# Forget attention, its output projection and the next input projection in one stage

## The chip, the cores and the metric

The kernel runs on one core of one Trainium2 chip, as one program of 18725 recorded instructions. The metric is the device time of one execution in microseconds (us); lower is better. Matrix products run on TensorE (PE, with its weight loads as PEld), elementwise work on VectorE (DVE) and ScalarE (ACT), a little on GpSimd (POOL), and the weight transfers are issued by SyncE (SP).

## The reference

Two stacks follow each other on a sequence of 256 tokens of width 1024 in float32: a two-layer one, and then four layers of the kinds fox, gla, gdn and fox again. Only the two fox layers and what follows them matter here. The mixer of such a layer is:

```python
def fox_mixer(xn, w_in, b_f, q_gain, k_gain, w_out):   # 8 heads of 128
    q, k, v, z, f_logit = split(xn @ w_in)              # 4 * 1024 + 8 columns
    q, k = rms_norm(q, q_gain), rms_norm(k, k_gain)
    cum = cumsum(log_sigmoid(f_logit + b_f), axis=1)
    logits = q @ k.T * scale + (cum[q_pos] - cum[k_pos]), -inf above the diagonal
    p = softmax(logits)
    return ((p @ v) * silu(z)) @ w_out
# the layer: x = x + mixer(rms_norm(x, norm_w)); the next layer: rms_norm(x) @ w_in of gla
```

After the second fox layer x is the result.

## The kernel before, in words

The 256 tokens are two tiles of 128 (`NT` = 2, tile t holds tokens 128t to 128t+127). `core.x` holds the residual stream on chip, and PSUM has 8 banks of 512 float32 columns for each partition.

**Products.** Every large projection is computed to near float32 accuracy from split operands: a weight and an activation are each the sum of a high part (a cast by ACT, `split_hi`, L188) and a low part (a subtraction by DVE, `split_lo`, L197), and `products` (L209 to L211) issues three matmuls, high by high, low by high and high by low. A weight comes in chunks of at most 4 x 128 rows by 512 columns, in the order in which `plan_weights` lists them. Three raw slots (`NRAW`) and three split slots (`NSPL`) exist. `issue` on SP's queue starts the transfer of a chunk when the chunk three places ahead of it has been split; `split_hi` waits for the landing, and for the products of the chunk three places back (`used`). The output projection is 4 chunks: two blocks of 512 columns, two halves of the 1024 rows each.

**Stages.** The program is a chain of stages; `core.stage` opens a block in which each engine has its own instruction list and waits on semaphores, and at its end all engines meet (L260). Around a fox layer they are:

- the stage that ends with the layer's input projection (`stage_ffn` for the first fox layer, `stage_seam` for the second). `Rest` runs its 9 blocks of 456 columns: PE multiplies, ACT moves each block out of PSUM with a scale (L934). The small steps of the layer (norms of q and k, their transposes, the gates) are hung into this loop by `fox_sides`. z is the last 1024 columns, so it lies in blocks 6 to 8.
- `stage_fox_attend`. It has four units, tile 0 heads 0 to 3, tile 0 heads 4 to 7, and the same for tile 1. Of each: PE makes the logits (L2513), DVE adds the gates and takes the row maxima (L2556) and negates them (L2561), ACT takes the exponentials with their sums (L2596), PE transposes them (L2540), DVE copies the transposes to SBUF (L2584), PE multiplies by v (L2525), DVE divides by the sums (L2570) and multiplies by silu(z) (L2575). ACT begins the stage with silu over all of z (L2591). The order on PE is written out: logits one unit ahead, values one unit behind. A unit of tile 0 sees 128 keys, a unit of tile 1 sees 256.
- the seam (`stage_seam`), for the first fox layer with the gla input projection, or `stage_last` for the second. `Turned` transposes the result of both tiles (L503), keeps PE running with three unused matmuls (`keep_warm`, L204), and ACT and DVE split the transposes in high and low (L512, L520), between the splits of the first two weight chunks. Then `Out` multiplies both blocks; its residual additions are DVE's (L579). In a seam, `Rms.pe` puts the transposes of x (L625) among products: those of tile 0 among the last products of the output projection, those of tile 1 among the first of the next projection. ACT and DVE scale and split them (L640, L647), after which `block` multiplies tile 0 and then tile 1 of the first block. ACT's list then has the squares of x (L669), POOL's power for the norm (L678), and the next weight splits.

The waits that set the order in the seam are these few:

```python
core.issue(sp, out.job[-1][-1]["g"] + 1)            # SP: the 4 chunks of the output projection
sp.wait_ge(sem("y_turn"), KD // 2)
core.issue(sp, body.job[-1][-1]["g"] + 1 + NRAW)    # then the next projection's, and 3 more
```

Of the kernel before, what the change touches and what calls it, by code (L numbers as in the profile page):

```python
# [72 lines left out]
class Core:  # L73


    def __init__(self, nc, a, ctx):
# [31 lines left out]
        self.chunks, self.jobs, self.mod = [], {}, {}  # L108
        self.issued = 0
# [347 lines left out]
class Splits:  # L457


    def __init__(self, core, names):  # L460
        self.core = core
        self.hi, self.lo = core.split_rings()
        self.chunks = [c for name in names for blk in core.jobs[name] for c in blk]
        self.at = {c["g"]: n for n, c in enumerate(self.chunks)}
        self.done = {"act": 0, "dve": 0}
# [129 lines left out]
class Norm:  # L595
# [3 lines left out]
    def __init__(self, core, tag, out, name, at):  # L599
        self.core, self.tag, self.out, self.job, self.split = core, tag, out, core.jobs[name], out.split  # L600
        self.hi, self.lo = core.act_pair()
        self.base = out.base
# [25 lines left out]
    def block(self, pe, sem, between):  # L628
        core, s = self.core, self.split
        core.mm_tiles(pe, self.job[0], s.hi, s.lo, self.hi, self.lo, lambda t: core.ps[:, 2 * self.base + t, :], 2, None,  # L630
# [50 lines left out]
class Rms(Norm):  # L681
# [8 lines left out]
    def pe(self, pe, sem):  # L690
# [6 lines left out]

        def second(t, i, j):
# [4 lines left out]
        self.out.pe(pe, sem, first)  # L703
        self.block(pe, sem, second)
# [25 lines left out]
class LnRms(Norm):  # L730
# [15 lines left out]
    def pe(self, pe, sem):  # L746
# [9 lines left out]
        self.core.keep_warm(2, 2 * self.base + 1)  # L756
# [43 lines left out]
class Ln(Norm):  # L800
# [17 lines left out]
    def pe(self, pe, sem):  # L818
# [9 lines left out]
        self.core.keep_warm(2, 2 * self.base + 1)  # L828
# [72 lines left out]
class Rest:  # L901


    def __init__(self, core, norm, dst, side, scaled):
        self.core, self.norm, self.dst, self.side, self.scaled = core, norm, dst, side, scaled
        self.split, self.job = norm.split, norm.job
# [5 lines left out]
    def bank(self, n, t):  # L912
        return 2 * ((self.norm.base + n) % 2) + t
# [11 lines left out]
    def act(self, act, sem):  # L925
        self.norm.act(act, sem)
        if self.scaled:
            act.wait_ge(self.norm.s(sem, "rms"), 1)
        for n, blk in enumerate(self.job):
            self.split.act(act, self.split.last(blk) + NSPL)  # L930
            act.wait_ge(self.core.used, blk[-1]["idx"] + 1)
            for t in range(NT):
                scale = self.norm.rs[:, t:t + 1] if self.scaled else 1.0
                self.core.nc.scalar.activation(self.dst(n, t), self.core.ps[:, self.bank(n, t), 0:blk[0]["width"]], ACT.Copy,  # L934
                                               scale=scale).then_inc(sem("taken"), 1)
            self.run("act", n, act, sem)

# [11 lines left out]
class Gated:  # L949
# [10 lines left out]
    def bank(self, n, t):  # L960
        return self.core.ps[:, 2 * ((self.norm.base + n) % 2) + t, :]
# [70 lines left out]
def stage_seam(core, before, name, scale, at, dst, side):  # L1032
# [4 lines left out]
    split = Splits(core, (prev, name))  # L1037
    out = Out(core, "y", split, prev, Turned(core, split, y))
    body = Rest(core, Rms(core, "m", out, name, scale, at), dst, side, True)
# [2578 lines left out]
```

## Time and profile before

| | |
|---|---|
| median of three runs | 1575.83 us (1567.4, 1575.83, 1576.15) |
| profiled execution, its own time | 1573.45 us |
| span of its trace | 1571.7 us |
| PE busy | 1435.2 us, 91% of the span |
| PEld, DVE, ACT, POOL busy | 73%, 56%, 44%, 14% |
| mean granted TensorE clock | 0.951 of full speed |
| products of the large projections, L209 to L211, x1216 each | 471.3, 461.4 and 462.4 us busy |
| weight splits, L188 on ACT and L197 on DVE, x176 each | 316.3 and 407.3 us busy |

The span is the time from the first to the last recorded instruction; 1.75 us of the execution lie outside it. Busy times of PE are recorded lengths that overlap (the next matmul enters before the last has left), so durations worked out from PE are taken from starts, not from recorded lengths. The granted clock is 1.00 at 2.4 GHz and 0.50 at 1.2 GHz.

### The profile page before, as it was taken

What the parts mean: (1) busy time and instruction counts of PE and PEld (TensorE: products, weight loads), DVE (VectorE), ACT (ScalarE), POOL (GpSimd) and SP (SyncE); (2) the same over time, 40 slices, a digit from 0 to 9 for tenths busy, and PEclk for the clock granted to TensorE, in tenths of its full rate; (3) what the DMA queues carried; (4) which work ended last, traced back from release to release, by engine and by line L of the source; (5) the groups of instructions that cost most, each with busy time, mean ns of one, the idle gap of its engine ahead of it and who ended that gap; (6) DMA issues with size and microseconds to landing.
All of it is one profiled execution on the core that took longest, in us unless ns stands there. A gap on an engine that the chain in (4) does not pass through costs nothing. (4 is left out here: it accounts for less than half of the span.)

```text
span 1571.7 us, 18725 instructions
## 1 busy us (share of the span) xinstructions
PE 1435.2 (91%) x7434; PEld 1145.8 (73%) x7434; DVE 875.7 (56%) x1179; ACT 689.4 (44%) x985; POOL 214.4 (14%) x119
## 2 busy tenths in 40 slices
PE   6999999999999988889999989979999974979988
PEld 2684668777888765567888868968886974868976
DVE  0755792667554553456755455646436577365635
ACT  1432432155443445346444335545543773236542
POOL 0003532103000040211200000200000032310300
PEclk7999799899999998799999999999999997989999
DMA  9655363165565463815666438805523530028821
GB/s 328 213 172 177 134 237 139 47 222 187 188 214 175 147 200 104 291 47 160 214 188 214 161 119 184 225 10 169 171 95 121 191 133 15 1 71 185 214 95 54
DMA packets 157155, 244.10 MB, mean 155 GB/s; under 512 B 14070, under 2 KB 95946, under 8 KB 156556
## 3 DMA queue, kind: packets, MB, share of 16 engines
q1 hardware_dynamic: 155916, 237.56, 48.4%
q0 software_dynamic: 1152, 5.34, 0.9%
q8 instruction: 59, 0.97, 0.2%
q14 instruction: 28, 0.23, 0.0%
HBM read 241.77 MB, written 1.11 MB: 155 GB/s over the span
## 5 line engine op out<-in xcount | busy, mean ns | idle before, releaser
L197 DVE TENSOR_TENSOR w_lo<-w_raw,w_hi 128x2048 fp32r<-128x2048 f32 (+3 forms) x176 | 407.3, 2324 | 273.0 <-ACT w_hi L188 272.9
L209 PE MATMUL ps<-w_hi,act_hi 128*128 128x512 f32 (+4 forms) x1216 | 471.3, 388 | 8.4 <-DVE act_lo L520 3.3
L211 PE MATMUL ps<-w_hi,act_lo 128*128 128x512 f32 (+4 forms) x1216 | 462.4, 380 | 0.0
L210 PE MATMUL ps<-w_lo,act_hi 128*128 128x512 f32 (+4 forms) x1216 | 461.4, 379 | 0.0
L188 ACT CAST w_hi<-w_raw 128x2048 fp32r<-128x2048 f32 (+3 forms) x176 | 316.3, 1803 | 293.9 <-PE ps L211 212.7
L209 PEld LDWEIGHTS ps<-w_hi,act_hi 128*128 128x128 f32 x1216 | 230.1, 189 | 53.3 <-issue 12.9
L211 PEld LDWEIGHTS ps<-w_hi,act_lo 128*128 128x128 f32 x1216 | 229.5, 189 | 37.3
L210 PEld LDWEIGHTS ps<-w_lo,act_hi 128*128 128x128 f32 x1216 | 230.0, 189 | 35.6 <-issue 1.4
L318 PE MATMUL ps<-w_raw,condz 128*32 128x512 f32 x384 | 63.7, 771 | 19.2 <-DMA w_raw<-in_ada_w 15.1
L934 ACT ACTIVATE proj<-ps,nstat 128x456 f32<-128x456 f32 (+2 forms) x64 | 37.1, 632 | 88.3 <-PE ps L211 88.3
L209 PE MATMUL ps<-w_hi,ffn_gh 128*128 128x512 f32 x176 | 70.2, 399 | 0.0
L211 PE MATMUL ps<-w_hi,ffn_gl 128*128 128x512 f32 x176 | 69.7, 396 | 0.0
L210 PE MATMUL ps<-w_lo,ffn_gh 128*128 128x512 f32 x176 | 69.7, 396 | 0.0
L204 PE MATMUL ps<-con 128*128 128x512 f32 x96 | 50.5, 673 | 18.3 <-DVE up L3413 18.3
L664 POOL TENSOR_TENSOR nstat<-nstat,con 128x1 f32<-128x1 f32 x8 | 5.4, 678 | 432.9 <-DVE nstat L659 432.9
L204 PEld LDWEIGHTS ps<-con 128*128 128x128 f32 x96 | 20.5, 226 | 39.1 <-issue 39.0
L326 PEld LDWEIGHTS ps<-con,ada_part 128*128 128x128 f32 x192 | 31.2, 247 | 23.6 <-issue 18.8
L336 ACT COPY ada_part<-ps 128x512 f32<-128x512 f32 x24 | 14.0, 583 | 74.4 <-PE ps L318 74.4
L1003 ACT ACTIVATE ffn_s<-ps 128x256 f32<-128x256 f32 x44 | 14.5, 381 | 68.9 <-PE ps L211 68.9
L318 PEld LDWEIGHTS ps<-w_raw,condz 128*32 128x32 f32 x384 | 10.3, 122 | 45.9 <-DMA w_raw<-in_ada_w 25.3
L211 PEld LDWEIGHTS ps<-w_hi,ffn_gl 128*128 128x128 f32 x176 | 33.2, 189 | 7.9
L210 PEld LDWEIGHTS ps<-w_lo,ffn_gh 128*128 128x128 f32 x176 | 33.2, 189 | 7.6
(478 smaller groups left out, 1838.6 us busy)
## 6 DMA issues: line engine op xcount, KB each, us to landing
w_raw<-in_ada_w SPq DMA_DIRECT2D x48, 1024.0 KB, 6.7
w_raw<-in_ffn_w_in SPq DMA_DIRECT2D x88, 512.0 KB, 4.9
w_raw<-in_fox_w_in SPq DMA_DIRECT2D x32, 912.0 KB, 9.1
w_raw<-in_ffn_w_out SPq DMA_DIRECT2D x20, 1024.0 KB, 5.1
w_raw<-in_rwkv_w_rkv SPq DMA_DIRECT2D x12, 1024.0 KB, 5.2
w_raw<-in_gla_w_in SPq DMA_DIRECT2D x10, 896.0 KB, 4.8
w_raw<-in_gdn_w_in SPq DMA_DIRECT2D x10, 896.0 KB, 5.0
w_raw<-in_fox_w_out SPq DMA_DIRECT2D x8, 1024.0 KB, 5.0
```

The lines of the kernel that those rows point to most:

```text
L188: self.nc.scalar.copy(hi[:, s, 0:c["nk"], 0:c["width"]], self.raw[:, c["slot"], 0:c["nk"], 0:c["width"]]).then_inc(self.hi_done, 1)
L197: self.nc.vector.tensor_tensor(lo[:, s, 0:c["nk"], 0:c["width"]], self.raw[:, c["slot"], 0:c["nk"], 0:c["width"]], hi[:, s, 0:c["nk"], 0:c ...
L204: self.nc.tensor.matmul(self.ps[:, bank, :], self.c("ident"), moving, start=True, stop=True)
L209: nc.tensor.matmul(out(t)[:, 0:w], xh[:, k, tok], hi[:, s, j, 0:w], start=start, stop=False)
L210: nc.tensor.matmul(out(t)[:, 0:w], xh[:, k, tok], lo[:, s, j, 0:w], start=False, stop=False)
L211: return nc.tensor.matmul(out(t)[:, 0:w], xl[:, k, tok], hi[:, s, j, 0:w], start=False, stop=stop)
L318: r = core.nc.tensor.matmul(self.sums[32 * j:32 * j + 32, :], core.condz[:, k, :], core.raw[:, c["slot"], j, :], start=(k < KG), stop=(k > ...
L326: r = core.nc.tensor.matmul(self.turned[:, 4 * n + j:4 * n + j + 1], self.part[n % 2][:, j * P:j * P + P], core.c("ones")[:, 0:1], start=T ...
L336: core.nc.scalar.copy(self.part[n % 2][:, :], self.sums).then_inc(sem("ada_part"), 1)
L664: self.core.nc.gpsimd.tensor_tensor(self.rs[:, t:t + 1], self.ve[:, t:t + 1], self.core.c("mhalf")[:, 0:1], ALU.pow).then_inc(self.s(sem, ...
L934: self.core.nc.scalar.activation(self.dst(n, t), self.core.ps[:, self.bank(n, t), 0:blk[0]["width"]], ACT.Copy, scale=scale).then_inc(sem( ...
L1003: nc.scalar.activation(self.act_s[:, n % 2, t, :], self.bank(n, t)[:, 0:T], ACT.Silu).then_inc(sem("silu"), 1)
```

## The change: one stage in place of two, and another order in it

`stage_fox_attend` is removed. Its work becomes a class, `FoxMix`, whose lists for PE, ACT and DVE are run at the head of the stage of the output projection (`stage_seam` or `stage_last`). What differs:

- All four units have logits buffers of their own (`lg` has 4 places in place of 2). PE issues the logits of all four first, then turns and values.
- `Tiles` takes the place of `Turned`: the attention's result is transposed, and split in high and low, one token tile at a time. `OutTiles` takes the place of `Out`: it multiplies in parts, one part being one chunk for one token tile (12 matmuls). Parts (0, tile 0), (1, tile 0) and (2, tile 0) stand among the attention of tile 1; the other five follow. PSUM banks are dealt out by tile.
- The first two chunks of the output weight are split already in the stage before (`ahead`), the third at the head of ACT's list in the new stage, and at the end of the mixer's DVE list.
- silu(z) is applied as the input projection is moved out of PSUM (`Rest.act`, blocks 6 to 8; block 6 is cut in two), and L2591 is gone. ACT begins the new stage with an exponential of one column.
- The transposed exponentials of the last unit are copied by ACT, not DVE.
- In the gla seam the transposes of x for tile 0 stand after all products of the output projection, followed by two unused matmuls (`keep_warm`), no longer among the last products. `OutTiles` ignores `between`.

```diff
 class Splits:
-    def __init__(self, core, names):
+    def __init__(self, core, names, ahead=None):
...
+        taken = core.ahead.pop(names[0], 0)
+        if taken:
+            self.hi, self.lo = core.rings
+        core.rings = self.hi, self.lo
+        if ahead is not None:
+            self.chunks += [c for blk in core.jobs[ahead] for c in blk][:2]
+            core.ahead[ahead] = 2
...
 class Rms(Norm):
...
         self.out.pe(pe, sem, first)
+        if tiled:
+            pe.wait_ge(x, NT + 1)
+            self.turn(pe, sem, self.core.x, 0)
+            self.core.keep_warm(2, self.out.bank(0, 1))
         self.block(pe, sem, second)
...
 class Rest:
...
+                if plain:
+                    r = self.core.nc.scalar.activation(out[:, 0:plain], ps[:, 0:plain], ACT.Copy, scale=scale)
+                if plain < w:
+                    r = self.core.nc.scalar.activation(out[:, plain:w], ps[:, plain:w], ACT.Silu, scale=scale)
+                r.then_inc(sem("taken"), 1)
...
+class Tiles:
+    def turn(self, pe, sem, t):
+        for h in range(2):
+            for j in range(4):
+                k = 4 * h + j
+                r = nc.tensor.transpose(ps[:, self.banks[t] + h, j * P:j * P + P], self.src[:, t, k * P:k * P + P], core.c("ident"))
+            r.then_inc(sem("y_turn"), 1)
...
+class OutTiles(Out):
+    def bank(self, n, t):
+        return 2 * (1 - t) + n % 2
+
+    def part(self, pe, sem, m, t):
+        core, s, c, y = self.core, self.split, self.list[m], self.src
+        if t == 0:
+            pe.wait_ge(core.lo_done, c["idx"] + 1)
+        pe.wait_ge(sem("y_lo"), 2 * t + m % 2 + 1)
+        for j in range(KG):
+            r = core.products(c, j, t, s.hi, s.lo, y.hi, y.lo, lambda t: core.ps[:, self.bank(m // 2, t), :],
+                              m % 2 == 0 and j == 0, m % 2 == 1 and j == KG - 1)
...
+    def pe(self, pe, sem, between=None):
+        for m in range(3):
+            self.part(pe, sem, m, 1)
+        self.part(pe, sem, 3, 0)
+        self.part(pe, sem, 3, 1)
+
+    def dve(self, dve, sem):
+        dve.wait_ge(self.s(sem, "tile0"), 1)
+        self.residual(dve, sem, 0, 0)
+        self.split.dve(dve, self.e1 + 1)
+        dve.wait_ge(self.core.used, self.list[1]["idx"] + 1)
+        self.residual(dve, sem, 0, 1)
+        self.split.dve(dve, self.e1 + 2)
...
 def stage_seam(...):
-            sp.wait_ge(sem("y_turn"), KD // 2)
+            sp.wait_ge(sem("y_turn"), 4)
...
+class FoxMix(Mixer):
+    def pe(self, pe, sem, out):
+        for n in range(3):
+            self.logits(pe, sem, n)
+        pe.wait_ge(sem("max"), 8)
+        self.logits(pe, sem, 3)
+        self.turn(pe, sem, 0)
+        self.turn(pe, sem, 1)
+        self.values(pe, sem, 0)
+        self.values(pe, sem, 1)
+        self.turn(pe, sem, 2)
+        pe.wait_ge(sem("max"), 16)
+        pe.wait_ge(sem("oz"), 2)
+        self.y.turn(pe, sem, 0)
+        self.values(pe, sem, 2)
+        self.turn(pe, sem, 3)
+        out.part(pe, sem, 0, 0)
+        self.values(pe, sem, 3)
+        out.part(pe, sem, 1, 0)
+        pe.wait_ge(sem("oz"), 4)
+        self.y.turn(pe, sem, 1)
+        out.part(pe, sem, 2, 0)
+
+    def act(self, act, sem, split):
+        nc.scalar.activation(sm[:, 31:32], self.core.c("ones")[:, 0:1], ACT.Exp)
+        split.act(act, 3)
...
+        self.y.high(act, sem, 0, 0)
+        self.y.high(act, sem, 0, 1)
+        self.moved(act, nc.scalar.copy, sem, 3)
+        self.y.high(act, sem, 1, 0)
+        self.y.high(act, sem, 1, 1)
+
+    def dve(self, dve, sem, split):
+        for n in range(4):
+            top(n)
+        self.moved(dve, nc.vector.tensor_copy, sem, 0)
+        self.moved(dve, nc.vector.tensor_copy, sem, 1)
+        scaled(0)
+        scaled(1)
+        self.moved(dve, nc.vector.tensor_copy, sem, 2)
+        self.y.low(dve, sem, 0, 0)
+        self.y.low(dve, sem, 0, 1)
+        scaled(2)
+        scaled(3)
+        split.dve(dve, 3)
+        self.y.low(dve, sem, 1, 0)
+        self.y.low(dve, sem, 1, 1)
```

## Rows read from the trace of the kernel before

**Rows 1.** Busy time by stretch, from logits to products, and the last projection's products

```profile
core 0: us, PE busy (x) PEld busy (x) DVE busy (x) ACT busy (x) POOL busy (x), PEclk, DMA share, GB/s
1032.44:1062.33 29.89, 20.27 (x127) 16.85 (x127) 18.45 (x56) 17.36 (x42) 0.00 (x0) 0.94 0.02 2
...
1516.62:1546.57 29.95, 20.33 (x127) 16.66 (x127) 18.44 (x56) 17.35 (x42) 0.00 (x0) 0.94 0.00 1
1546.57:1568.61 22.04, 22.04 (x96) 17.92 (x96) 9.71 (x8) 3.79 (x3) 0.00 (x0) 1.00 0.22 83
```

**Rows 2.** The same view, three stretches of the first attention, for PEclk

```profile
1034.46:1038.62 4.16, 0.01 (x1) 0.00 (x0) 1.26 (x12) 4.13 (x11) 0.00 (x0) 0.99 0.01 2
1038.62:1042.47 3.85, 3.85 (x12) 3.27 (x13) 0.69 (x1) 1.49 (x8) 0.00 (x0) 0.56 0.00 0
1049.00:1062.33 13.33, 9.19 (x63) 7.28 (x63) 9.53 (x15) 6.80 (x13) 0.00 (x0) 1.00 0.04 3
```

**Rows 3.** Timeline, PE, first attention: start us, us, engine, line, operation

```profile
1032.44 2.02 PE L2513 MATMUL ps<-kt,qt 128*128 128x128 f32 x16 [1.51 <-PEq L260]
...
1039.53 3.10 PE L2513 MATMUL ps<-kt,qt 128*128 128x256 f32 x8
...
1043.80 1.89 PE L2513 MATMUL ps<-kt,qt 128*128 128x256 f32 x8
```

**Rows 4.** Timeline, DVE, first attention

```profile
1033.61 0.29 DVE L2556 CUSTOM_DVE_ANT_0 lg<-ps,gate 128x128 f32<-128x128 f32 x1 [15.54 <-PE ps L2513]
...
1034.66 0.28 DVE L2556 CUSTOM_DVE_ANT_0 lg<-ps,gate 128x128 f32<-128x128 f32 x1
...
1042.67 0.42 DVE L2556 CUSTOM_DVE_ANT_0 lg<-ps,gate 128x256 f32<-128x256 f32 x1 [2.20 <-PE ps L2513]
...
1044.25 0.68 DVE L2584 COPY pt<-ps 128x512 f32<-128x512 f32 x1
...
1045.12 0.69 DVE L2570 TENSOR_TENSOR proj<-ps,sm 128x512 f32<-128x512 f32 x1
...
1045.85 0.69 DVE L2575 TENSOR_TENSOR proj<-proj 128x512 f32<-128x512 f32 x1
...
1048.03 1.23 DVE L2584 COPY pt<-ps 128x1024 f32<-128x1024 f32 x1
```

**Rows 5.** Timeline, ACT, around the first attention

```profile
1030.97 1.17 ACT L934 ACTIVATE proj<-ps,nstat 128x456 f32<-128x456 f32 x2 [8.27 <-PE ps L211]
...
1035.63 1.28 ACT L2596 ACT_TABLE_LOAD   x1
1036.92 0.40 ACT L2596 ACTIVATE lg<-lg,mx 128x128 f32<-128x128 f32 x1
...
1044.38 0.51 ACT L2596 ACTIVATE lg<-lg,mx 128x256 f32<-128x256 f32 x1 [4.27 <-DVE mx L2561]
```

**Rows 6.** Timeline, ACT and DVE, head of the gla seam

```profile
1056.76 1.90 ACT L188 CAST w_hi<-w_raw 128x2048 fp32r<-128x2048 f32 x1 [6.53 <-PEq L260]
1058.56 1.07 ACT L512 CAST act_hi<-ps 128x512 fp32r<-128x512 f32 x2
...
1058.69 2.29 DVE L197 TENSOR_TENSOR w_lo<-w_raw,w_hi 128x2048 fp32r<-128x2048 f32 x1 [2.29 <-ACT w_hi L188]
...
1060.90 1.28 DVE L520 TENSOR_TENSOR act_lo<-ps,act_hi 128x512 fp32r<-128x512 f32 x2
```

**Rows 7.** Timeline, from the last products of the output projection into the gla projection

```profile
1080.13 1.03 PE L625 MATMUL ps<-con,x_res 128*128 128x128 f32 x8
...
1080.77 2.17 ACT L640 ACTIVATE act_hi<-ps,cols 128x128 fp32r<-128x128 f32 x8 [5.49 <-PE ps L625]
...
1081.94 2.16 DVE L647 SCALAR_TENSOR_TENSOR act_lo<-ps,cols,act_hi 128x128 fp32r<-128x128 f32 x8 [2.29 <-ACT act_hi L640]
...
1086.97 2.17 ACT L640 ACTIVATE act_hi<-ps,cols 128x128 fp32r<-128x128 f32 x8 [2.45 <-PE ps L625]
...
1093.94 3.96 DVE L197 TENSOR_TENSOR w_lo<-w_raw,w_hi 128x1792 fp32r<-128x1792 f32 x2 [2.54 <-ACT w_hi L188]
```

More of the change, by code:

```diff
@@ L108, in __init__ @@
         self.chunks, self.jobs, self.mod = [], {}, {}
+        self.ahead, self.rings = {}, None
         self.issued = 0
@@ L755, in pe @@
         self.turn(pe, sem, self.core.x, 0)
-        self.core.keep_warm(2, 2 * self.base + 1)
+        self.core.keep_warm(2, self.out.bank(0, 1))
         self.block(pe, sem, between)
@@ L827, in pe @@
         self.turn(pe, sem, self.xn, 0)
-        self.core.keep_warm(2, 2 * self.base + 1)
+        self.core.keep_warm(2, self.out.bank(0, 1))
         self.block(pe, sem, between)
@@ L901, with __init__ @@
 class Rest:
[L904 to L905 removed]
+    def __init__(self, core, norm, dst, side, scaled, silu=None):
+        self.core, self.norm, self.dst, self.side, self.scaled, self.silu = core, norm, dst, side, scaled, silu
         self.split, self.job = norm.split, norm.job
@@ L912, in bank @@
     def bank(self, n, t):
-        return 2 * ((self.norm.base + n) % 2) + t
+        return self.norm.out.bank(n, t)
     def pe(self, pe, sem):
@@ L928, in act @@
             act.wait_ge(self.norm.s(sem, "rms"), 1)
+        at = 0
         for n, blk in enumerate(self.job):
+            w = blk[0]["width"]
+            plain = w if self.silu is None else max(0, min(w, self.silu - at))
             self.split.act(act, self.split.last(blk) + NSPL)
@@ L960, in bank @@
     def bank(self, n, t):
-        return self.core.ps[:, 2 * ((self.norm.base + n) % 2) + t, :]
+        return self.core.ps[:, self.norm.out.bank(n, t), :]
     def turn(self, pe, sem, n):
@@ L1040, in stage_seam @@
+def stage_seam(core, before, name, scale, at, dst, side, silu=None, ahead=None):
+    prev, y = before
+    split = Splits(core, (prev, name), ahead)
+    mixer = y if isinstance(y, Mixer) else None
+    if mixer is None:
+        out = Out(core, "y", split, prev, Turned(core, split, y))
+    else:
+        out = OutTiles(core, split, prev, mixer.y)
+    body = Rest(core, Rms(core, "m", out, name, scale, at), dst, side, True, silu)
     with core.stage(f"{prev}_{name}") as (block, sem):
@@ L1050, in _ @@
         def _(pe):
+            if mixer is not None:
+                mixer.pe(pe, sem, out)
             body.pe(pe, sem)
@@ L1054, in _ @@
         def _(act):
+            if mixer is not None:
+                mixer.act(act, sem, split)
             body.act(act, sem)
@@ L1058, in _ @@
         def _(dve):
+            if mixer is not None:
+                mixer.dve(dve, sem, split)
             body.dve(dve, sem)
@@ L1063, in _, with stage_ffn @@
             body.pool(pool, sem)
-def stage_ffn(core, l, before, name, dst, side, scale=None, at=None):
+def stage_ffn(core, l, before, name, dst, side, scale=None, at=None, silu=None, ahead=None):
     prev, y = before
@@ L1085, in stage_ffn @@
         norm = LnRms(core, "n", back, name, (l, 1), scale, at, ln)
-    body = Rest(core, norm, dst, side, scale is not None)
+    body = Rest(core, norm, dst, side, scale is not None, silu)
     with core.stage(f"{prev}_{name}") as (block, sem):
@@ L1120, in stage_last @@
 def stage_last(core, before):
-    prev, y = before
+    prev, mixer = before
     split = Splits(core, (prev,))
-    out = Out(core, "y", split, prev, Turned(core, split, y))
+    out = OutTiles(core, split, prev, mixer.y)
     core.at_end = True
@@ L1139, in _ @@
         def _(pe):
+            mixer.pe(pe, sem, out)
             out.pe(pe, sem)
```

221 lines of the change are left out of this document (118 added, 103 removed).

## The prediction

> **What bounds the kernel now.** I read the page's first part first: PE is busy 91% of the span, so a change can win only where PE idles, works on nothing useful or runs at half clock. Then the busy times by stretch around both fox layers, to see where the 9% lies; then the timeline of each engine there. The windows show it: from the first logits to the first product of the output projection 29.89 us pass in one layer and 29.95 in the other, with PE busy 20.3 of them and some of that on unused matmuls; the 96 products of the last projection then take 22.04 us with no gap, so 2.75 us for each part of 12 [rows 1]. The attention is a chain DVE, ACT, PE, DVE, PE of small steps. Ahead of the first transposes PE stands still for 4.16 us, and the 3.85 us behind that run at a granted clock of 0.56, so mostly at 1.2 GHz; the 13.33 us at the end of the attention and the head of the seam also hold several pauses, and there the clock stays at 1.00 [rows 2]. Eight logit matmuls of 256 keys take 3.10 us in the slow piece and 1.89 later [rows 3]. Behind the attention stand a meeting of engines, 16 transposes, three unused matmuls and four splits, two of weights and two of activations, before the first product (group 6 shows those of ACT and DVE). So both layers have a stretch where PE has work only for part of the time, while 22 us of products wait for data that, for tile 0, is ready early.
>
> **The change part by part.** I lay out the new stage, in us from the first logits (1032.44 and 1516.62 before), with the old durations.
>
> 1. *Logits and maxima.* The first DVE operation starts 1.17 after the logits; a unit of tile 0 takes DVE 1.05 and one of tile 1 1.58, from the starts of neighbours [rows 4]. Logits of units 0 and 1 end on PE at 2.0, of unit 2 at 3.9, and those of unit 3 wait for eight maxima (3.3), which costs nothing, and end at 5.7 (1.89 each [rows 3]). DVE: 1.17 to 3.27 for units 0 and 1, 3.95 to 5.5 and 5.7 to 7.25 for the others.
>
> 2. *Exponentials.* ACT's list begins with one table load (1.28), a small exponential (0.2; no row shows it, between 0.1 and 0.4), and the third weight chunk's cast (1.90 [rows 6]), ready at 3.4. Before, a table load for silu, silu itself and a second table load held the first exponential to 4.48 [rows 5, 3], so this is 1.1 earlier. Units of 128 keys take 1.6, of 256 keys 2.0 [rows 5]: ends at 5.0, 6.6, 8.6 and 10.6. None is the last thing waited for. A rule of the Trainium skill (ScalarE: Activation LUTs, What ACT_TABLE_LOAD costs) adds a drain of 1.38 us to each load of 1.28. The trace disagrees here: the first exponential starts 1.29 after the load starts [rows 5]. By the rule the second copy on DVE would come 0.7 later, and the sum would lose 1.4 us over both layers.
>
> 3. *Transposes and values of tile 0.* PE turns units 0 and 1 at 5.7 to 7.2. DVE copies them after its maxima, 7.25 to 8.5 (0.6 to 0.7 each); values run at 7.95 to 9.0 and to 9.95. DVE then divides and gates: 0.87 from a copy to the division, 0.73 to the gating, 0.61 on [rows 4]. That makes two gated halves at 10.4 and 12.05, and the unit-2 copy (1.23) at 13.25. PE waits for the second half: transposes of tile 0 at 12.1 to 13.1 (8 take 1.03 [rows 7]). The largest pause of PE up to here is 1.1 us.
>
> 4. *The interleaved part.* From 13.25 the order on PE is full: values of unit 2 (16 matmuls, 1.9, to 15.1), turns (1.0, 16.1), part 0 of tile 0 (2.75, 18.9), values of unit 3 (1.9, 20.7), part 1 (23.5), transposes of tile 1 (1.0, 24.5), part 2 (27.2). What each waits for is there: ACT's two casts of tile 0 (0.54 each from 1.07 for two [rows 6]) end at 13.9, DVE's subtractions (0.64 each) at 14.6; ACT's copy of unit 3, of which no row exists, is due between 1.1 (two casts of the same total width) and 1.9 (the weight cast of double width), at 17.3 to 18.1 against 18.9. DVE's split of the third chunk (2.29) ends at 24.4 against 24.5: no slack, and a few tenths may show.
>
> 5. *The last five parts* take 5 x 2.75 and end at 41.0. The fourth weight chunk can be cast once part 0 of tile 1 is done (30.0) and is split at 34.3, wanted at 35.5. Its transfer is now issued at the head of the stage, since the chunk ahead of it is split already. SP's wait for the tile-1 transposes has behind it the gla chunks; before it passed about 26 us after the first logits, now at about 24.5, and the first gla chunk is wanted only at 33. These transfers cost nothing.
>
> 6. *Second fox layer.* Before, 29.95 + 22.04 = 52.0 [rows 1]; now 41.0. The final addition and output transfers keep their places. Gain 11.0.
>
> 7. *First fox layer.* The transposes of x for tile 0 lose their cover: they begin after the last part, 41.0. By the distances of before, scaling starts 0.64 later, its low parts 1.17 after that and take 2.16 [rows 7]; only then does DVE add the second half of tile 1 (0.69, like the division that also reads 512 columns of PSUM [rows 4]) and PE turns it, and ACT begins on it 0.64 later: 41.0 + 0.64 + 1.17 + 2.16 + 0.69 + 0.64 = 46.3. Before, ACT began on it at 1086.97, which is 54.5. From there on the order is the same (squares, norm, the next weight splits, the last of which ended at 1097.9), and that chain of ACT and DVE, not PE, releases the second gla block. Gain 8.2. The two unused matmuls (1.8) lie within the 2.9 us of waiting. The pieces between are the loss of the moved transposes, 2.8.
>
> 8. *Early splits and silu in the stage before.* Two casts of 1.90 and two subtractions of 2.29. ACT idles 8.27 us ahead of its last move [rows 5] and DVE 15.54 behind its last split [rows 4]; the second cast waits for the middle of the last block's products and is ready 3.3 before their end, the subtraction 1.1 before. Silu goes at the same rate as a copy, block 6 pays one table load and two short operations (1.9 us), and PE wants its bank ten microseconds later. All hidden. If the cover were gone, 1 to 2 us a layer.
>
> Sum: 11.0 + 8.2 = 19.2. New handovers cost about 0.05 each in the timeline, ten to a layer where PE or DVE is last, of which I take 0.5 in all: **18.7 us**. The profiled execution took 1573.45, so 1554.8; the median was 2.4 higher, so **1557.1**.
>
> **The rivals.** *Clock episodes remain (gain about 15).* The long idle piece goes, but PE at the start of the stage is still in pieces. One slow piece like that of before [rows 2] would cost 1.9 us in a layer, two layers 3.8: 1561. Against: pauses up to 1.8 us at full clock in the same attention.
>
> *No overlap (gain about 4).* If the parts of tile 0 find their operands late (PE's list is strictly written, one late wait holds all behind it), only the removed boundary is won. The old way from the last gating (1056.4) to the first product (1062.33) is 5.9; turn, cast and subtraction are 2.3, so 3.6 a layer, less the 2.8 of point 7: 4.4 in all, 1571.4. Against: each operand above has its row, and only one has no slack.
>
> *Slower: half clock through the interleaving.* Many short bursts instead of one long idle piece. The Trainium skill (TensorE: Matmul & The Clock Gate, A second HAM failure mode: psum-queue depth-cycling) warns of just this: frequent small idles between groups make the clock swing. As a mechanism of this kernel: between 7.95 and 27.2 PE has about 15.5 us of work; at half clock that is doubled, less 3 us of pauses that it fills, so 12.5 a layer, and 25 against 19: 1576 + 6 = 1582. It decides from 9.4 us lost in each layer. Against: the pauses at the end of the old attention left the clock at 1.00 [rows 2], and the trace so far does not bear the rule out.
>
> *More than forecast:* the clock falls elsewhere too (mean 0.951), and later stages could meet it differently; the runs before differ by 9 us. A gain over 22 needs that.
>
> **How the numbers follow.** Forecast (gain 16 to 22) 0.62; clock episodes, or small waits of the same size (10 to 16) 0.19; no overlap (below 10, not slower) 0.07; slower 0.04; more (over 22) 0.08. One per cent, about what this measurement can tell from no change, is 15.8 us. Above it lie the forecast, the case of more and a little of the episodes: 0.71. Within it 0.25, slower by more 0.04. The range reaches from 8 us of gain to 28: 1548 to 1568; it takes in the bounds of points 2, 4 and 8, the episodes, and part of the run-to-run difference, and leaves out the two worst cases and the extremes.
>
> **What the profile should show.** First to last product of the second layer: logits to last product 41 us (52 before); in the first layer 46 us to the second group of scalings (54.5). No L2591, one table load at the head of the stage, exponentials from 3.4. PE's pause before the first transposes under 0.5 in place of 4.16, and a granted clock of 1.00 throughout. Between part 3's products and the gla block a new gap of about 2.9 with two L204 in it. The input projections unchanged in length. The prediction is wrong if PE waits on the third chunk's low part, on ACT's copy, or at a clock of 0.5; or if the moved transposes cost more than 2.8.

## The result and the profile after

The changed kernel takes **1556.1 us** (median of 4 runs, 1555.42 to 1558.42), the kernel before 1575.92 in the same comparison (4 runs, 1567.4 to 1576.15). The ratio is 0.9892, 95% interval 0.9864 to 0.9919: faster by 1.1%. The median is 1.0 us from the predicted 1557.1. The profiled execution took 1555.56 us with a span of 1553.9, so 1.7 lie outside the span, as before.

The page's first line and first part:

```profile
span 1553.9 us, 18677 instructions
...
PE 1428.2 (92%) x7426; PEld 1140.0 (73%) x7426; DVE 872.9 (56%) x1177; ACT 689.2 (44%) x991; POOL 214.4 (14%) x119
```

PE still is busiest, 92% of the span, and its busy time fell by 7 us only: most unused matmuls and the half-clock pieces of the two fox layers are gone. The rest of the gain is idle time of PE. Busy times by stretch: from the first logits to the end of the last product of the output projection, for the first and for the second fox layer, and last the thinnest piece of the first.

```profile
core 0: us, PE busy (x) PEld busy (x) DVE busy (x) ACT busy (x) POOL busy (x), PEclk, DMA share, GB/s
1034.02:1074.90 40.88, 38.06 (x216) 32.57 (x217) 24.47 (x61) 17.02 (x42) 0.00 (x0) 1.00 0.36 114
1509.66:1550.70 41.04, 38.22 (x216) 32.42 (x216) 22.53 (x60) 15.34 (x41) 0.00 (x0) 1.00 0.13 46
1039.33:1046.22 6.89, 4.18 (x34) 3.50 (x32) 6.06 (x19) 4.96 (x22) 0.00 (x0) 1.00 0.00 0
```

The first two rows answer to [rows 1], where the same work took 29.95 + 22.04 us with PE idle for 9.6. Now it takes 40.88 and 41.04 with 2.8 idle, and nearly all of that lies in the third row, where units 0 and 1 go through DVE. The clock column answers to [rows 2]: 1.00 in place of 0.56 behind the first transposes. The timeline of PE, first fox layer; in brackets the idle time ahead of a row and what ended it:

```profile
1034.02 5.48 PE L2649 MATMUL ps<-kt,qt 128*128 128x128 f32 x32 [1.51 <-PEq L261]
1039.33 0.60 PE L2660 MATMUL ps<-con,lg 128*128 128x128 f32 x4
1040.40 0.66 PE L2660 MATMUL ps<-con,lg 128*128 128x128 f32 x4 [0.47 <-ACT lg L2706]
1041.85 2.05 PE L2672 MATMUL ps<-proj,pt 128*128 128x128 f32 x16 [0.79 <-DVE pt L2721]
1043.74 1.04 PE L2660 MATMUL ps<-con,lg 128*128 128x128 f32 x8
1046.22 1.06 PE L1071 MATMUL ps<-con,proj 128*128 128x128 f32 x8 [1.44 <-DVE proj L2748]
1047.26 2.05 PE L2672 MATMUL ps<-proj,pt 128*128 128x128 f32 x16
1049.15 1.04 PE L2660 MATMUL ps<-con,lg 128*128 128x128 f32 x8
1049.94 0.48 PE L210 MATMUL ps<-w_hi,act_hi 128*128 128x512 f32 x1
...
1052.79 1.95 PE L2672 MATMUL ps<-proj,pt 128*128 128x128 f32 x16
...
1057.30 1.03 PE L1071 MATMUL ps<-con,proj 128*128 128x128 f32 x8
...
1074.90 1.03 PE L632 MATMUL ps<-con,x_res 128*128 128x128 f32 x8
1075.77 1.88 PE L205 MATMUL ps<-con 128*128 128x512 f32 x4
1077.99 0.44 PE L210 MATMUL ps<-w_hi,act_hi 128*128 128x448 f32 x1 [0.33 <-DVE act_lo L654]
```

Three pauses are left, 0.47, 0.79 and 1.44. From the transposes of tile 0 (L1071, 1046.22) on, PE has no gap in brackets until the output projection is through: part 0 starts at 15.92 us from the first logits, between the turns of unit 3 and its values. One short wait hides there: part 2 starts 1.15 us behind the start of the transposes of tile 1 (1057.30 to 1058.45), part 0 only 0.79 behind the start of eight transposes of the same size (1049.15 to 1049.94). The last three rows are the price in the first layer: nothing covers the x transposes (L632), and two unused matmuls (L205, recorded as four) fill most of the wait. The timeline of ACT in the same layer:

```profile
1033.98 1.28 ACT L2700 ACT_TABLE_LOAD   x1 [0.27 <-PEq L261]
1035.27 0.20 ACT L2700 ACTIVATE sm<-con 128x1 f32<-128x1 f32 x1
1035.38 1.88 ACT L189 CAST w_hi<-w_raw 128x2048 fp32r<-128x2048 f32 x1
1037.17 0.40 ACT L2706 ACTIVATE lg<-lg,mx 128x128 f32<-128x128 f32 x1
...
1050.22 1.02 ACT L2721 COPY pt<-ps 128x1024 f32<-128x1024 f32 x1 [2.27 <-PE ps L2660]
...
1075.54 2.18 ACT L647 ACTIVATE act_hi<-ps,cols 128x128 fp32r<-128x128 f32 x8 [6.85 <-PE ps L632]
...
1080.21 2.18 ACT L647 ACTIVATE act_hi<-ps,cols 128x128 fp32r<-128x128 f32 x8 [0.92 <-PE ps L632]
```

One table load, and the first exponential 3.15 us behind the logits. The second row of L647 is the scaling of tile 1 of x, 46.19 us from the first logits; it answers to 1086.97 in [rows 7], which was 54.53. And the timeline of DVE: the split of the third chunk, the low parts of tile 1, the scaled low parts, the residual of tile 1, and the last addition of the kernel.

```profile
1056.11 2.28 DVE L198 TENSOR_TENSOR w_lo<-w_raw,w_hi 128x2048 fp32r<-128x2048 f32 x1
1058.56 1.29 DVE L1086 TENSOR_TENSOR act_lo<-ps,act_hi 128x512 fp32r<-128x512 f32 x2 [0.16 <-ACT act_hi L1082]
...
1076.71 2.16 DVE L654 SCALAR_TENSOR_TENSOR act_lo<-ps,cols,act_hi 128x128 fp32r<-128x128 f32 x8 [3.65 <-ACT act_hi L647]
1078.79 0.67 DVE L587 TENSOR_TENSOR x_res<-x_res,ps 128x512 f32<-128x512 f32 x1
...
1550.76 0.69 DVE L587 TENSOR_TENSOR x_res<-x_res,ps 128x512 f32<-128x512 f32 x1 [2.03 <-PE ps L212]
```

**The books.** I read two local figures in every kernel, both from that layer's first logits: in the first fox layer the start of ACT's second scaling of x, in the second the start of the last addition. They went from 54.53 to 46.19 and from 52.03 to 41.10: gains of 8.34 and 10.93, together 19.27. The span fell by 17.8. Nearly all of the difference is upstream: the first logits of the first layer start at 1034.02, not 1032.44, 1.58 later. Yet the distance to them from DVE's last split of the input projection's weight is 16.44 after and 16.43 before, and from the move of the first block that holds part of z (block 6, ACT) 23.26 and 23.25. So silu and the two more splits in that stage are hidden, and the 1.58 arose earlier.

### The profile page after: what moved, and what is told of

Read it like the earlier page. It is cut to its first block and busy times, and to the rows that moved or that the text cites. A ratio compares the mean times of both kernels' runs of the same rounds, so it can differ in the third digit from the quotient of the medians.

```text
span 1553.9 us, 18677 instructions
## 1 busy us (share of the span) xinstructions
PE 1428.2 (92%) x7426; PEld 1140.0 (73%) x7426; DVE 872.9 (56%) x1177; ACT 689.2 (44%) x991; POOL 214.4 (14%) x119
## 5 line engine op out<-in xcount | busy, mean ns | idle before, releaser
L205 PE MATMUL ps<-con 128*128 128x512 f32 x88 | 46.4, 674 | 18.3 <-DVE up L3578 18.3
L952 ACT ACTIVATE proj<-ps,nstat 128x456 f32<-128x456 f32 (+3 forms) x56 | 32.3, 625 | 66.4 <-PE ps L212 66.4
L327 PEld LDWEIGHTS ps<-con,ada_part 128*128 128x128 f32 x192 | 30.6, 243 | 24.4 <-issue 20.4
L205 PEld LDWEIGHTS ps<-con 128*128 128x128 f32 x88 | 18.9, 227 | 37.9 <-issue 37.8
```

Of the source, the lines that this page charges most:

```text
L205: self.nc.tensor.matmul(self.ps[:, bank, :], self.c("ident"), moving, start=True, stop=True)
L327: r = core.nc.tensor.matmul(self.turned[:, 4 * n + j:4 * n + j + 1], self.part[n % 2][:, j * P:j * P + P], core.c("ones")[:, 0:1], start=T ...
L952: r = self.core.nc.scalar.activation(out[:, 0:plain], ps[:, 0:plain], ACT.Copy, scale=scale)
```

## The experiments

All are read by the two local figures first. Times in us. The runs fall into five rounds, and each ratio is against runs of the kernel before in its own round, whose medians lie between 1572.17 and 1575.92; medians of different rounds are not to be compared.

| run | first layer | second layer | median (range, runs) | ratio, 95% |
|---|---|---|---|---|
| before | 54.53 | 52.03 | 1575.92 (1567.4 to 1576.15, 4) | |
| after | 46.19 | 41.10 | 1556.1 (1555.42 to 1558.42, 4) | 0.9892, 0.9864 to 0.9919 |
| parts_late | 48.89 | 43.77 | 1558.57 (1555.06 to 1562.25, 7) | 0.9914, 0.9889 to 0.9939 |
| no_ahead | 48.12 | 43.04 | 1558.26 (1553.52 to 1560.91, 6) | 0.9903, 0.9872 to 0.9934 |
| silu_head | 49.38 | 43.78 | 1558.94 (1557.35 to 1563.24, 5) | 0.9918, 0.9885 to 0.9951 |
| x_cover | 44.86 | 41.10 | 1553.99 (1551.83 to 1554.96, 4) | 0.9882, 0.9835 to 0.9928 |
| before_warm | 52.87 | 50.30 | 1568.68 (1562.2 to 1581.18, 10) | 0.9983, 0.9954 to 1.0013 |
| silu_only | 52.27 | 48.17 | 1564.82 (1556.67 to 1569.77, 10) | 0.9942, 0.992 to 0.9964 |
| two_stages | 52.12 | 47.00 | 1564.67 (1556.91 to 1570.28, 10) | 0.9945, 0.9923 to 0.9967 |
| no_warm | 47.29 | 41.13 | 1550.08 (1545.77 to 1558.89, 4) | 0.9855, 0.9818 to 0.9891 |
| x_cover2 | 44.16 | 41.06 | 1553.85 (1545.46 to 1554.75, 6) | 0.9862, 0.9834 to 0.989 |
| fused | 43.28 | 40.20 | 1546.0 (1543.61 to 1552.72, 6) | 0.9825, 0.9795 to 0.9855 |
| after_again | 46.18 | 41.07 | 1550.33 (1549.24 to 1558.73, 5) | 0.9868, 0.9846 to 0.9889 |
| fused_again | 43.29 | 40.19 | 1550.4 (1544.61 to 1560.1, 6) | 0.9859, 0.9829 to 0.9889 |

My theory was that four things make the gain: products of tile 0 in the attention's gaps, no boundary between attention and products, weight splits done ahead, and a shorter head of the attention (silu moved, clock kept). The rival was that one of them makes nearly all of it, the clock above all.

**parts_late**: same stage, same split order, but no products among the attention of tile 1.

```diff
-        out.part(pe, sem, 0, 0)
         self.values(pe, sem, 3)
-        out.part(pe, sem, 1, 0)
         pe.wait_ge(sem("oz"), 4)
         self.y.turn(pe, sem, 1)
+        out.part(pe, sem, 0, 0)
+        out.part(pe, sem, 1, 0)
```

> The changed kernel, with the first two parts of tile 0 moved from among the attention to behind the transposes of tile 1. Theory of the hand schedule: PE then idles about 1.2 us for ACT's copy and 1.6 us for DVE's last division and gating, and nothing else is lost, because all of tile 0 is ready before tile 1; so 41.0 us from first logits to last product become 43.8, 2.8 us a layer, 5.6 in all, about 1561.7. Rival, that interleaving carries the gain: two parts of 2.75 us are uncovered in each layer, 5.5 a layer, 11 in all, about 1567.

It lost 2.70 and 2.67, close to the expected 2.8. PE now waits 1.10 for ACT's copy and 1.51 for DVE's last gating. The placing among the attention is worth 2.7 a layer, a quarter of the gain of the second layer, not half.

**no_ahead**: the first two chunks of the output weight are split in the new stage.

```diff
-        split.act(act, 3)
+        split.act(act, 2)
...
+        split.act(act, 3)          # behind both casts of tile 0
...
+        split.dve(dve, 1)
         scaled(2)
+        split.dve(dve, 2)
         scaled(3)
```

> The changed kernel without the splits of two output chunks in the stage before: ACT casts chunks 0 and 1 at the head of its list and chunk 2 behind the first casts of the attention's result, DVE subtracts them behind tile 0's subtractions and around its divisions. Hand schedule: the two subtractions of 2.3 us lie on DVE between tile 0's subtractions and the divisions that PE waits for; part 0 starts near 16.9 in place of 15.9 after the logits, and the rest shifts with it: 1 to 2 us a layer, about 1559. Rival, the early splits are what removed the fill of the old seam: 3.5 us or more a layer, about 1563 or more.

It lost 1.93 and 1.94. PE's timeline has the place: part 0 waits for the first low part of the weight, 17.8 us from the logits in place of 15.9.

```profile
1046.82 0.50 PE L210 MATMUL ps<-w_hi,act_hi 128*128 128x512 f32 x1 [0.86 <-DVE w_lo L198]
```

**silu_head**: silu goes back to the head of ACT's list; DVE waits for it ahead of the gating.

```diff
-        nc.scalar.activation(sm[:, 31:32], self.core.c("ones")[:, 0:1], ACT.Exp)
+        nc.scalar.activation(self.w["z"][:, :, :], self.w["z"][:, :, :], ACT.Silu).then_inc(sem("z"), 1)
...
+            dve.wait_ge(sem("z"), 1)
```

> The changed kernel with silu(z) again as one operation at the head of ACT's list, and copies alone in the moves out of PSUM. Hand schedule: exponentials start at 6.3 us after the logits in place of 3.2, DVE's first copies wait for them, the second gated half of tile 0 is 1.6 to 1.8 us later, and nothing later absorbs that: 3.4 us in both layers, about 1559.5. Rival, ACT is not on the path since no exponential was waited for last: no change, 1556.

It lost 3.19 and 2.68. The exponentials start 6.26 after the logits, which was in the working; what follows was not. Busy times, in the first layer, of PE's pause ahead of the first transposes and of the values behind it:

```profile
core 0: us, PE busy (x) PEld busy (x) DVE busy (x) ACT busy (x) POOL busy (x), PEclk, DMA share, GB/s
1037.01:1039.50 2.49, 0.00 (x1) 0.01 (x1) 1.64 (x9) 2.48 (x10) 0.00 (x0) 1.00 0.00 0
1041.78:1045.00 3.22, 3.22 (x18) 3.22 (x18) 2.01 (x4) 3.13 (x14) 0.00 (x0) 0.55 0.00 0
```

A pause of 2.49 us, four transposes still at full speed (0.65), a pause of 0.88, and then the engine goes to 1.2 GHz: 16 value matmuls take 3.33 us, 2.05 in the changed kernel. The second layer has the same two pauses and 3.28. The loss exceeds the expected 1.7 a layer by 1.5 and 1.0; the slow values, 1.3 and 1.2, are of that size. Why the two layers differ by 0.5 was not traced.

**before_warm**: the kernel before, with unused matmuls in its long pause, to have the clock's share alone.

```diff
                 if n + 1 < len(units):
                     logits(pe, n + 1)
+                if n == 0:
+                    core.keep_warm(4, 6)
```

> The kernel before with four unused matmuls (about 3.5 us) in the long pause of PE ahead of the attention's first transposes. They end before the exponentials are ready (4.16 us of pause). If the slow clock behind the pause is the pause's doing, the granted clock stays at 1.00, the eight logit matmuls of 256 keys take 1.9 us in place of 3.1 and the transposes 0.6 in place of 1.1: 1.3 to 1.7 us a layer, about 3 in all, 1573. Rival: the slow piece costs nothing because DVE and ACT set the pace there: no change, 1576.

It gained 1.66 and 1.73; the granted clock from 1037.50 to 1042.00 is 1.00, and it is 1.00 in the same place of the second layer too. So 1.7 a layer of the old time was half clock. The timed ratio does not tell 3.4 us from nothing; the local figures do.

```profile
1037.50:1042.00 4.50, 4.30 (x28) 3.97 (x29) 2.54 (x11) 1.86 (x11) 0.00 (x0) 1.00 0.00 0
```

**silu_only**: the kernel before, with silu applied in the stage before and the exponential of one column at the head.

```diff
...
+                if plain < w:
+                    r = self.core.nc.scalar.activation(out[:, plain:w], ps[:, plain:w], ACT.Silu, scale=scale)
...
-            nc.scalar.activation(w["z"][:, :, :], w["z"][:, :, :], ACT.Silu).then_inc(sem("z"), 1)
+            nc.scalar.activation(sm[:, 31:32], core.c("ones")[:, 0:1], ACT.Exp)
```

> The kernel before with only the silu of z moved into the moves out of PSUM, and a table load by a one-column exponential. The first exponential starts 2.3 us after the logits in place of 4.5; the pause of PE shrinks to about 2 us, and the slow clock behind it goes too: 2.2 plus 1.3 to 1.7 us a layer, 7 to 8 in all, about 1568.5. Rival, the clock falls all the same, or DVE takes the exponentials' place: 2 to 4 in all, about 1573.

It gained 2.26 and 3.86: the expectation holds in the second layer alone. PE's timeline of both layers, the first transposes and the logits behind them:

```profile
1040.72 0.66 PE L2548 MATMUL ps<-con,lg 128*128 128x128 f32 x4 [2.02 <-ACT lg L2603]
1041.22 3.43 PE L2521 MATMUL ps<-kt,qt 128*128 128x256 f32 x8
...
1520.83 0.66 PE L2548 MATMUL ps<-con,lg 128*128 128x128 f32 x4 [2.02 <-ACT lg L2603]
1521.32 1.89 PE L2521 MATMUL ps<-kt,qt 128*128 128x256 f32 x8
```

The granted clock of both pieces, from the first transposes on:

```profile
1040.72:1044.65 3.93, 3.92 (x13) 3.15 (x14) 0.69 (x1) 1.49 (x8) 0.00 (x0) 0.59 0.00 0
1520.83:1523.21 2.38, 2.38 (x14) 2.13 (x15) 0.69 (x1) 1.49 (x8) 0.00 (x0) 1.00 0.01 3
```

The same pause of 2.02, once with the half clock behind it and once without. In the slow case the four transposes still take 0.66, and only the logits behind them are slow. The difference, 1.54, is all but the whole difference of the two gains (1.60).

**two_stages**: the attention with its new order, but in a stage of its own; the seam has both transposes of the result, then all eight parts. Splits ahead and silu stay.

```diff
     def pe(self, pe, sem, out):
+        self.y.turn(pe, sem, 0)
+        self.y.turn(pe, sem, 1)
+        for m in range(3):
+            out.part(pe, sem, m, 0)
...
+    with core.stage(f"fox{i}_attend") as (block, sem):
```

> The changed kernel with its stage cut in two again: the attention with its new order and the early silu in one, the transposes by tile and the parts in the next; the early splits of two chunks stay. Hand schedule: last gating 20.8 us after the logits, boundary 0.3, transposes of tile 0 half 0.6, cast 0.55, subtraction 0.65, first product near 23.0, then 22.0 of parts and 1.0 of transposes: last product 46.1 against 41.0, 5 us a layer. The order alone, parts behind the attention, was 2.7 of it; so the boundary and the fill behind it are 2.4. Rival, the boundary itself costs little, as the fill was already gone with the early splits: 3 us a layer.

It lost 5.93 and 5.90, of which parts_late says 2.7 are the interleaving. The timeline of PE, first layer:

```profile
1044.66 3.53 PE L2672 MATMUL ps<-proj,pt 128*128 128x128 f32 x16 [2.48 <-DVE pt L2728]
...
1054.15 1.94 PE L1071 MATMUL ps<-con,proj 128*128 128x128 f32 x16 [1.77 <-PEq L261]
```

and the granted clock behind the first of these pauses:

```profile
1044.66:1048.20 3.54, 3.54 (x17) 3.54 (x18) 0.03 (x1) 0.00 (x0) 0.00 (x0) 0.54 0.00 0
```

The meeting of engines costs PE 1.77. Where the changed kernel has the transposes of tile 0 this one has a pause of 2.48, and then 16 value matmuls in 3.53. The second layer has the same pause and a granted clock of 0.59 behind it. If the slow piece (about 1.5) shows in full at the end, the loss without it would be 4.4, under the 5 expected; no run took it out. In the changed kernel no pause of that length is left, and the clock stays at 1.00.

**no_warm**: the two unused matmuls ahead of the gla projection are left out.

```diff
-            self.core.keep_warm(2, self.out.bank(0, 1))
```

> The changed kernel without the two unused matmuls in the gla seam; PE then stands still 2.0 us between the transposes of x and the first gla product. Pauses of 2.0 us left the clock up once and were followed by 1.2 GHz once in another kernel. If it stays at 1.00: no change. If it falls: the first gla products are half as fast for some 3 to 4 us, 1.5 to 2 us longer, visible only between the second scaling (46.2 in both) and the end of the block.

It lost 1.10 in the first layer and nothing in the second (0.03), which has none of them. Busy times of the pause and what follows:

```profile
core 0: us, PE busy (x) PEld busy (x) DVE busy (x) ACT busy (x) POOL busy (x), PEclk, DMA share, GB/s
1066.73:1068.79 2.06, 0.01 (x2) 0.04 (x1) 1.28 (x5) 2.06 (x8) 0.00 (x0) 1.00 0.00 0
1068.79:1072.50 3.71, 3.71 (x15) 3.34 (x15) 3.41 (x6) 1.75 (x3) 0.00 (x0) 0.54 0.00 0
```

The eight transposes of x, tile 1, take 1.76 in place of 1.10, and each product ahead of them 0.57 in place of 0.36. They stand ahead of the second scaling, so the loss shows there; I had expected it only behind it. Yet the ratio of this kernel, 0.9855, is below the 0.9892 of after, and in its profile the first logits start as early as 1024.76. That run is why the table is read by its local columns.

**x_cover**: the transposes of x for tile 0 go back among the last products, to pay less than the 2.8 of the moved ones. The two unused matmuls go.

```diff
-            self.turn(pe, sem, self.core.x, 0)
-            self.core.keep_warm(2, self.out.bank(0, 1))
...
         self.part(pe, sem, 3, 0)
-        self.part(pe, sem, 3, 1)
+        self.part(pe, sem, 3, 1, between)     # turns x, tile 0, behind its second row block
```

> The changed kernel with the transposes of x for tile 0 again among the products of the last part, as the old seam had them, and without the two unused matmuls. Hand schedule: the scaling of tile 1 begins 43.3 us after the logits in place of 46.2, and the second gla block follows it: 2.8 us less in the first fox layer alone, about 1553.3. Rival, the splits of the gla chunks or their transfers release the next block, and the wait only moves: no change.

It gained 1.33, half of the 2.8 expected. PE and DVE, timeline:

```profile
1074.81 1.03 PE L632 MATMUL ps<-con,x_res 128*128 128x128 f32 x8
...
1077.89 0.44 PE L210 MATMUL ps<-w_hi,act_hi 128*128 128x448 f32 x1 [0.66 <-DVE act_lo L654]
...
1079.42 1.09 PE L632 MATMUL ps<-con,x_res 128*128 128x128 f32 x8
...
1076.62 2.16 DVE L654 SCALAR_TENSOR_TENSOR act_lo<-ps,cols,act_hi 128x128 fp32r<-128x128 f32 x8 [2.29 <-ACT act_hi L647]
1078.69 0.67 DVE L587 TENSOR_TENSOR x_res<-x_res,ps 128x512 f32<-128x512 f32 x1
```

Six products are left behind the transposes, shorter than the chain of ACT and DVE, so PE still pauses for 0.66. And the residual of tile 1 stands on DVE's list behind both halves of the low parts, so PE turns tile 1 only at 1079.42. I had priced the cover and not the queue.

**x_cover2**: one row block earlier, and the residual between the two halves.

```diff
+            if (t, i, j) == (1, 0, 0):        # was (1, 0, 1)
...
         self.scaled_low(dve, sem, self.scale, 0, 0)
+        self.out.tile(dve, sem, 1)
         self.scaled_low(dve, sem, self.scale, 0, 1)
```

> The run with the covered transposes of x gained 1.33 us from the logits to the second scaling (44.86 against 46.19), not 2.9. Its timeline shows why: with parts of 12 products only half a part was left as cover, so PE stood 0.66 us at the head of the gla block, and DVE added the second half of tile 1 only behind both of tile 0's subtractions. Here the transposes stand one row group of products earlier (after 3, not 6, products of the last part), and DVE adds tile 1's half between the two subtractions. If that is the cause: pause near 0.1, second scaling near 43.9 after the logits, 1549 to 1553 in all. Rival, the norm's chain or a weight split holds the next block whatever stands here: the scaling is earlier but the next block's first product is not.

It came to 44.16, 2.03 below after; 43.9 was expected. Some of it seems lost again: from there to ACT's next table load 43.68 us pass, 43.10 in the kernel after. A weight split of DVE is now waited for (0.23 at 1079.89), but fused has that wait too (0.24) and 43.17, so the cause of the rest is open.

**fused**: x_cover2, with division and gating in one instruction a head; four in place of two wide ones with a wait between. PE's values wait for the gating in place of the division.

```diff
...
+            for j in range(4):
+                r = nc.vector.scalar_tensor_tensor(o[:, t, c], ps[...], sm[...], w["z"][:, t, c], ALU.mult, ALU.mult)
```

> The previous kernel, and DVE's division and gating as one operation per head (PSUM times a per-row factor times z), four of 128 columns in place of two of 512 with a wait between. The changed kernel's longest pause of PE, 1.44 us, ends with the gating of tile 0's second half. Four operations take about 1.04 us in place of 1.34 plus the handover, so the half is ready 0.65 us earlier; PE's list is full from there: 0.65 us less in each layer, last addition 40.45 after the logits in place of 41.10, second scaling near 43.3. Rival, the copy of unit 2 or the turns release PE there: no change.

It gained 0.88 more in the first layer and 0.86 in the second. Timeline of DVE for units 0 and 1, and of PE:

```profile
1038.35 1.12 DVE L2745 SCALAR_TENSOR_TENSOR proj<-ps,sm,proj 128x128 f32<-128x128 f32 x4 [0.57 <-PE ps L2672]
...
1039.66 1.13 DVE L2745 SCALAR_TENSOR_TENSOR proj<-ps,sm,proj 128x128 f32<-128x128 f32 x4
...
1040.93 1.07 PE L1069 MATMUL ps<-con,proj 128*128 128x128 f32 x8 [0.85 <-DVE proj L2745]
```

The pause ahead of the transposes of tile 0 is 0.85, not 1.44: DVE was the last thing waited for there. That is 0.6, the size expected. The other 0.3 comes at part 2, which here starts 0.85 behind the start of the transposes of tile 1 (1052.01 to 1052.86) in place of 1.15 (1.14 in x_cover2): DVE reaches the split of the third chunk earlier, so PE no longer waits for its low part.

**after_again and fused_again**, side by side on one chip, to time the 3.8 us by which fused is locally ahead.

> The changed kernel again, beside the next run. By the profiles its median lies about 18.7 us under the kernel before, about 1554 to 1557, and the local figures repeat within 0.1 us: second scaling 46.2, last addition 41.1 after the logits. What lies ahead of the first logits should differ from profile to profile (1025 to 1037 so far), since it follows the granted clock there.

> The version with covered transposes of x and the fused gating, again. By the local figures it should lie 2.9 + 0.9 = 3.8 us under the changed kernel, about 1552; its first median was 10 us under. If that was more than the local gain, this time the difference is nearer to 3.8; rival, the edits gain elsewhere too and the difference is again 8 or more.

Every local figure came back within 0.03. The medians are 1550.33 and 1550.4: no difference was measured, and 1550.33 is below the 1554 to 1557 that I had expected for the changed kernel. In the two profiles the first logits start at 1031.48 and 1036.60; from there to the end of the span fused_again takes 514.2 and after_again 517.4. Both orders of the kernel are well below the kernel before; that fused is faster in total is argued from its local figures and not shown by the medians.

## Why the prediction was right, point by point

**Points 1 to 3** held to 0.4 us: first exponential 3.15 (3.4 forecast), turns of unit 0 at 5.31 (5.7), transposes of tile 0 at 12.20 (12.1). The largest pause is 1.44 and not 1.1: DVE's gating ended at 12.05 as laid out, but PE was through with the turns of unit 2 some 0.2 earlier than I had it, and its transposes began 0.1 later. The first activation again starts 1.29 after its table load: the trace disagrees with the drain of 1.38 us that the Trainium skill (ScalarE: Activation LUTs, What ACT_TABLE_LOAD costs) adds.

**Point 4.** Part 0 at 15.92 (16.1), values of unit 3 at 18.77 (18.9), transposes of tile 1 at 23.28 (23.5). ACT's copy of unit 3, without a row before, takes 1.02, just below the lower end of its range (1.1); it had slack either way. The low part of the third chunk ends at 24.37 (24.4), and part 2 starts at 24.43, some 0.3 later than it would behind ready operands (1.15 against 0.79 and 0.85 in the starts above). So PE does wait for the third chunk's low part, in both layers, which the prediction named as a sign of being wrong; point 4 also said that a few tenths might show there, and that is its size.

**Points 5 and 6.** Last product through at 40.88 and 41.04 (41.0). Gain in the second layer 10.93, forecast 11.0.

**Point 7.** Gain 8.34, forecast 8.2; second scaling at 46.19 (46.3). The loss by the moved transposes, taken as the difference of the two layers, is 10.93 - 8.34 = 2.6, forecast 2.8; x_cover2 gets 2.0 of it back. That the two unused matmuls lie in the wait is right, but they are not neutral: no_warm shows them worth 1.1. The sum had no term for that, and did not need one with them in place.

**Point 8.** Hidden: 16.44 against 16.43 from the input projection's last split to the logits, 23.26 against 23.25 from the move of block 6.

**The sum.** Local gains 19.27, above the 18.7, as the 0.5 for handovers was not needed; the span's 17.8 has the upstream 1.58 off it. The same kernel had a median of 1550.33 in a later round. That the total is within 1 us is therefore partly luck, and the agreement of the parts is the better evidence.

**The rivals.** *Clock episodes remain*: excluded by the clock of 1.00 in both stages. Its price of 1.9 a layer was near: before_warm gives 1.7. But the case was nearer than its chance says: silu_head and two_stages have a pause of about 2.5 us where the changed kernel has 1.44 at most, and both have the slow piece. *No overlap*: parts_late takes the overlap out and still gains (54.53 - 48.89) + (52.03 - 43.77) = 13.9 us, so this case, which I had put at 4.4 in all, left out the splits ahead and the shorter head. *Half clock through the interleaving*: the Trainium skill (TensorE: Matmul & The Clock Gate, A second HAM failure mode: psum-queue depth-cycling) warns of it; here pauses of 0.47, 0.79 and 1.44 us between short groups left the granted clock at 1.00 in both layers. My working of that case was wrong in size: between 7.95 and 27.2 the list of PE as laid out holds about 18 us of work and 1.3 of pauses, not 15.5 and 3, so half clock all through would have cost nearly 17 a layer, not 12.5. The forecast does not use it.

**Where the gain comes from.** Undone one at a time, in the second layer: interleaving 2.7, stage boundary with its slow piece 3.2 (two_stages less parts_late), splits ahead 1.9, silu 2.7. They come to 10.5 of 10.93, though nothing says that they must add up, and the boundary and silu terms each hold a slow piece (about 1.5 and 1.3). The rival that the clock makes nearly all of it falls: filled up alone in the old kernel it gives 1.7 a layer.

**Expectations that missed in size**: silu_head, silu_only (first layer) and two_stages by a slow piece of 1.3 to 1.5 that I had not put behind a pause of 2 to 2.5 us; x_cover by a queue order on DVE; fused by the 0.3 at part 2. no_warm missed the place: its loss shows already at the second scaling.

## What to carry to other kernels

When a chain of small steps precedes a block of products whose first half depends on an early part of the chain, join both in one stage and lay the list of each engine out with starts and ends from the rows; on this kernel the starts so worked out came within 0.4 us. Price a pause of TensorE of 2 us and more as the pause and a possible slow piece behind it (1.1 to 1.7 us here), and fill it with unused matmuls where nothing waits for them. Read an edit of a few us by a distance within its own stage, from a start that the edit does not touch, for the total moves by more than that with nothing changed.

## What was not expected of the hardware

The granted clock behind a pause is no function of the pause alone: 2.02 us was followed by 1.2 GHz once and by 2.4 GHz once, in the same kernel, with the same work around it. Pauses of 2.06, 2.48 and 2.49 us were followed by 1.2 GHz (with clocks of 0.54 and 0.55 in the rows above); those of up to 1.77 in these rows were not. Nor does the fall come with the first matmul behind the pause each time: in silu_only and silu_head the first four transposes still took 0.66 and 0.65, in the kernel before 1.12. What decides stays open.

The start of the first fox layer, behind a thousand us of nearly the same work, lies between 1024.8 and 1036.7 in the profiles of the kernels here, and even the kernel after shows 1034.02 and 1031.48. The granted clock differs upstream, as in the rows for 40 to 320 us of before and of after_again:

```profile
40.00:320.00 280.00, 266.74 (x1650) 190.83 (x1651) 173.77 (x240) 94.26 (x130) 67.63 (x34) 0.93 0.48 164
```

```profile
40.00:320.00 280.00, 264.36 (x1654) 190.74 (x1655) 174.80 (x239) 95.98 (x131) 67.38 (x34) 0.95 0.49 166
```

Nothing in that stretch is changed. Over all that lies ahead of the first logits the granted clock is 0.97 in no_warm, the earliest (1024.76), and 0.95 in silu_only and fused_again, the latest (1036.68 and 1036.60). But it is 0.97 in after_again too, with 1031.48, so the clock goes with part of the spread only. Why it differs there was not tried.
